# A two-layer hybrid decoder trunk: epilogues run one tile ahead, attention with a deeper lookahead, expert stages interleaved

## What is computed

```python
for l in range(2):
    sh1, sc1, g1, sh2, sc2, g2 = split(silu(c) @ ada_w[l] + ada_b[l])
    h = x * (1 + sc1) + sh1
    y = even_mixer(h) if l % 2 == 0 else odd_mixer(h)
    x = layer_norm(ALPHA * x + (1 + g1) * y)
    h = x * (1 + sc2) + sh2
    y = grouped_moe(h)          # 16 experts, top 2 of one group, d_ff 512
    x = layer_norm(ALPHA * x + (1 + g2) * y)

# even_mixer: concat(diff_attention, hgrn2) @ w_out;  odd_mixer: concat(rg_lru, stick_breaking) @ w_out
def diff_attention(q, k, v, lam, gain):      # 4 heads, two score maps per head, causal, ALiBi
    p = softmax(q @ k.T * scale - slope * dist)
    a = p[0] - lam * p[1]
    return rms_norm(a @ v, gain)

def grouped_moe(h):                           # every expert is computed, weighted by its gate
    for e in range(16):
        y += gates[:, e] * ((silu(h @ w_gate[e]) * (h @ w_up[e])) @ w_down[e])
```

## Time and profile before

| | us |
|---|---|
| five executions, median | 17749.61 |
| lowest and highest of them | 17496.92 and 18180.02 |
| the profiled execution | 17749.61 |
| its span (first to last instruction), slowest core 1 | 17748.1 |
| spans of the other cores | 17541.1 to 17740.6 |
| mean granted clock, cores 0 to 3 and 4 to 7 | 0.709 and 0.719 |

### The profile page before, as it was taken

How to read it: one execution, slowest core, us unless ns; L and a number is a source line. 1 busy time by engine, 2 the same in 40 slices (tenths; PEclk the granted TensorE clock), 3 DMA queues, 4 the chain that set the end, 5 groups by cost and what they waited for, 6 DMA issues and landing times.

```text
span 17748.1 us, 176812 instructions; the slowest of 8 cores (17541.1 to 17748.1 us)
## 1 busy us (share of the span) xinstructions
PE 12155.7 (68%) x42368; PEld 4591.4 (26%) x42368; DVE 6999.8 (39%) x11532; ACT 4772.7 (27%) x8362; POOL 3427.5 (19%) x3132
## 2 busy tenths in 40 slices
PE   5936666532958769497337678777844958949597
PEld 2311111311424334243113111111112423424243
DVE  1112222443333433333231677777743333333334
ACT  3233333300111111110431566666601111111111
POOL 0021111321222212122120122121121212212122
PEclk7967776765978878687568555555556868868798
DMA  5210000222433333232101000000012323323233
GB/s 113 81 57 8 8 1 8 80 66 58 72 68 60 58 64 58 50 65 50 54 6 39 17 9 1 8 2 8 2 65 59 64 62 53 50 63 59 63 60 60
DMA packets 603199, 811.71 MB, mean 46 GB/s; under 512 B 105994, under 2 KB 441994, under 8 KB 597516
## 3 DMA queue, kind: packets, MB, share of 16 engines
q0 software_dynamic: 362432, 446.20, 15.6%
q1 hardware_dynamic: 239760, 354.21, 6.5%
HBM read 1105.90 MB, written 138.47 MB: 70 GB/s over the span
## 4 chain that ended last, share of the span: by engine, by line
PE 48%; DVE 16%; ACT 11%; issue 8%; DMA 8%; POOL 7%; SPq 1%; DVEq 1%; ACTq 0%; POOLq 0%
PE ps L363 48%; ACT arena L312 10%; POOL arena L317 7%; DVE arena L317 6%; DVE arena L330 5%; DMA arena<-xs 2%; DVE arena L324 2%; DVE arena L346 1%; DMA arena<-x 1%; DVE arena L350 1%; DMA arena<-ada_w 1%; DVE arena L322 1%; DVEq L195 1%; DMA arena<-arena 1%; ACT L312 1%
## 5 line engine op out<-in xcount | busy, mean ns | idle before, releaser
L363 PE MATMUL ps<-arena 128*128 128x512 bf16 (+6 forms) x41280 | 11882.1, 440 | 3540.4 <-POOL arena L317 883.9
L363 PEld LDWEIGHTS ps<-arena 128*128 128x128 bf16 (+5 forms) x41280 | 4392.9, 116 | 11045.8 <-issue 8938.8
L317 POOL TENSOR_TENSOR arena<-arena 128x512 bf16<-128x512 bf16 (+3 forms) x2368 | 2989.5, 1266 | 12566.1 <-ACT arena L312 5867.8
L312 ACT ACTIVATE arena<-ps 128x512 bf16<-128x512 f32 (+2 forms) x3520 | 2022.9, 581 | 4227.1 <-PE ps L363 2933.7
L317 DVE TENSOR_TENSOR arena<-arena,ps 128x512 f32<-128x512 f32 x4096 | 2722.8, 685 | 841.7 <-PE ps L363 676.5
L312 ACT ACTIVATE arena<-arena 128x512 bf16<-128x512 f32 (+3 forms) x3013 | 1789.8, 594 | 3122.2 <-DVE arena L317 2517.6
L317 DVE TENSOR_TENSOR arena<-ps,arena 128x512 bf16<-128x512 f32 (+2 forms) x1272 | 878.1, 690 | 3768.1 <-PE ps L363 3746.1
L368 PE MATMUL ps<-arena 128*128 128x128 f32 x1088 | 273.6, 420 | 1923.0 <-DMA arena<-xs 1196.0
L330 DVE SCALAR_TENSOR_TENSOR arena<-ps,arena 128x512 f32<-128x512 f32 x1184 | 820.2, 693 | 562.5 <-ACT arena L312 540.1
L312 ACT ACTIVATE arena<-ps,arena 128x128 f32<-128x128 f32 (+2 forms) x1152 | 523.3, 460 | 1671.3 <-PE ps L368 1010.7
L317 DVE TENSOR_TENSOR arena<-arena 128x4 f32<-128x4 f32 (+6 forms) x1447 | 518.3, 388 | 991.4 <-ACT arena L312 409.7
(11 more groups left out here) (25 smaller groups left out, 928.0 us busy)
## 6 DMA issues: line engine op xcount, KB each, us to landing
arena<-moe_w_gate POOLq DMA_DIRECT2D x128, 1024.0 KB, 9.0
arena<-moe_w_up POOLq DMA_DIRECT2D x128, 1024.0 KB, 13.7
arena<-moe_w_down POOLq DMA_DIRECT2D x128, 1024.0 KB, 17.1
arena<-xs SPq DMA_DIRECT2D x192, 512.0 KB, 3.9
xs<-arena SPq DMA_DIRECT2D x96, 512.0 KB, 2.9
arena<-x SPq DMA_DIRECT2D x64, 512.0 KB, 4.1
arena<-ada_w POOLq DMA_DIRECT2D x12, 2048.0 KB, 19.1
out<-arena SPq DMA_DIRECT2D x32, 512.0 KB
```

Of the source, the lines that this page charges most:

```text
L312: self.P.op('scalar', lambda e: e.activation(out=o, in_=i, func=func, **kw), reads=_rs([in_, bias, scale]), writes=[out.r])
L317: self.P.op(eng, lambda e: e.tensor_tensor(out=o, in0=x, in1=y, op=op), reads=_rs([a, b]), writes=[out.r])
L363: self.P.op('tensor', lambda e: e.matmul(o, l, r, start=start, stop=stop), reads=_rs([lhsT, rhs] + list(xr)), writes=[out.r])
```

## The change

Four things change; what is computed does not.

Epilogues: `epilogue` is split into a load (`xload`), `epi_t1`, `epi_sums`, `epi_norm` and `epi_out`, and `epilogue_seq` runs them over the tiles so that gate product and sums of tile i + 1 stand between normalisation and output of tile i, with loads two tiles ahead out of a ring of three tiles (`xe_pool`). The square moves from POOL to ACT. Attention: three score banks (0, 1, 7) instead of two, probabilities three key blocks ahead instead of one, five `P` tiles instead of four; and the normaliser (`finish`) of a pair of blocks is issued inside the first block of the next pair. Experts: `stage2` of the item before no longer follows `stage1` as a whole; one of its four tiles follows each group `fc`.

```diff
-    xt_pool = b.pool([128, D], F32, 2, "xt")
+    xt_tiles = [b.sb([128, D], F32, "xt") for _ in range(2)]
+    def ring(tiles):
...
+    xt_pool = ring(xt_tiles)
...
-    def epilogue(xsrc, xdst, t0, y):
-        xe = xt_pool()
+    def xload(xsrc, t0):
+        xe = xe_pool[0]()
         b.dma('sync', xe, xsrc[t0:t0 + 128, :])
+        return xe
+
+    def epi_t1(y):
         t1 = ework[0]()
...
+    def epi_sums(xe, t0, t1):
         r = ework[1]()
-        b.stt('gpsimd', r, xe, ALPHA, t1, ALU.mult, ALU.add)
-        b.tt('gpsimd', t1, r, r, ALU.mult)
+        b.stt('vector', r, xe, ALPHA, t1, ALU.mult, ALU.add)
+        b.act(t1, r, AF.Square)
...
+    def epi_norm(ctx):
+        t0, xe, t1, r, st = ctx
         b.ts('vector', t1, r, st[:, 2:3], ALU.subtract, st[:, 6:7], ALU.mult)
         b.tt('gpsimd', r, t1, lnG, ALU.mult)
...
+    def epi_out(xdst, ctx):
+        t0, xe, t1, r, st = ctx
+        b.tt('vector', xe, r, lnB, ALU.add)
+        b.dma('sync', xdst[t0:t0 + 128, :], xe)
+
+    def epilogue_seq(xsrc, xdst, tiles, produce=None):
+        n = len(tiles)
+        xes = [xload(xsrc, tiles[0]), xload(xsrc, tiles[1])]
+        ctx = epi_sums(xes[0], tiles[0], epi_t1(produce(0)))
+        for i in range(n):
+            if i + 2 < n:
+                xes.append(xload(xsrc, tiles[i + 2]))
+            t1 = epi_t1(produce(i + 1)) if i + 1 < n else None
+            epi_norm(ctx)
+            nxt = epi_sums(xes[i + 1], tiles[i + 1], t1) if i + 1 < n else None
+            epi_out(xdst, ctx)
+            ctx = nxt
...
-                a = stage1(e, ch, wcur[e])
-                if prev is not None:
-                    stage2(*prev)
-                prev = (e, ch, wcur[e], a)
-            stage2(*prev)
-            for i in range(TH // 128):
-                epilogue(xsrc, xdst, tok0 + i * 128, yacc[:, i, :])
+                gbs, actT = stage1_begin(e, ch)
+                for fc in range(4):
+                    stage1_fc(e, ch, wcur[e], gbs, actT, fc)
+                    if prev is not None:
+                        stage2_tile(*prev, fc)
+                prev = (e, ch, wcur[e], actT)
+            for ti in range(4):
+                stage2_tile(*prev, ti)
+            epilogue_seq(xsrc, xdst, [tok0 + i * 128 for i in range(TH // 128)], lambda i: yacc[:, i, :])
...
-        p_pool = b.pool([128, 512], BF16, 4, "Pa")
+        p_pool = b.pool([128, 512], BF16, 5, "Pa")
...
+        pend = []
+
+        def finish(o, sq, h, qs):
+            ss = bank(6)
+            b.mm(ss, onesf, sq)
+            rstd = rl_pool()
+            b.rsqrt(rstd, ss, 128e-6, rstd)
+            b.stt('vector', BIG[:, h, qs], o, dgS, rstd, ALU.mult, ALU.mult)
...
-                        st = bank(J % 2)
+                        st = bank((0, 1, 7)[J % 3])
...
-                    P = s1(0)
-                    for J in range(nJ):
-                        Pn = s1(J + 1) if J + 1 < nJ else None
-                        b.mm(OT, vv[:, J, :], P, J == 0, J == nJ - 1)
-                        b.mm(LT, onesb, P, J == 0, J == nJ - 1)
-                        P = Pn
+                    Ps = {}
+                    for J in range(-3, nJ):
+                        if J + 3 < nJ:
+                            Ps[J + 3] = s1(J + 3)
+                        if J >= 0:
+                            P = Ps.pop(J)
+                            b.mm(OT, vv[:, J, :], P, J == 0, J == nJ - 1)
+                            b.mm(LT, onesb, P, J == 0, J == nJ - 1)
+                            if pend and J == min(6, nJ - 1):
+                                finish(*pend.pop())
...
-                ss = bank(6)
-                b.mm(ss, onesf, sq)
-                rstd = rl_pool()
-                b.rsqrt(rstd, ss, 128e-6, rstd)
-                b.stt('vector', BIG[:, h, qs], o, dgS, rstd, ALU.mult, ALU.mult)
+                pend.append((o, sq, h, qs))
+        finish(*pend.pop())
```

More of the change, by code:

```diff
@@ L488, in build, with nxt @@
     b.pop()
-    xt_pool = b.pool([128, D], F32, 2, "xt")
+    xt_tiles = [b.sb([128, D], F32, "xt") for _ in range(2)]
+    def ring(tiles):
+        k = [0]
+        def nxt():
+            k[0] += 1
+            return tiles[(k[0] - 1) % len(tiles)]
+        return nxt
+    xt_pool = ring(xt_tiles)
     hf_pool = b.pool([128, 8, 128], F32, 2, "hf")
@@ L574, in moe_sublayer @@
         r1 = b.pool([128, 1], F32, 8, "r1")
+        xe_pool[0] = ring(xt_tiles + [b.sb([128, D], F32, "xe")])
         def router(hf, col):
@@ L671, in stage1 @@
-                return actT
-            def stage2(e, ch, wts, actT):
-                wd = wts[2]
-                for ti in range(4):
-                    ycnt[0] += 1
-                    ya, yb = (PS[3][0], PS[3][1]) if ycnt[0] % 2 else (bank(4), bank(5))
-                    for nh, yp in ((0, ya), (1, yb)):
-                        for fc in range(4):
-                            b.mm(yp, actT[:, fc, ti * 128:(ti + 1) * 128], wd[:, fc, nh * 512:(nh + 1) * 512],
-                                 fc == 0, fc == 3)
-                    tix = ch * 4 + ti
-                    for nh, yp in ((0, ya), (1, yb)):
-                        ys = yacc[:, tix, nh * 512:(nh + 1) * 512]
-                        if e == 0:
-                            b.cp('vector', ys, yp)
-                        else:
-                            b.tt('vector', ys, ys, yp, ALU.add)
+                return gbs, act_pool()
@@ new lines, in stage1_fc @@
+            def stage1_fc(e, ch, wts, gbs, actT, fc):
+                wg, wu, wd = wts
+                c0 = ch * 512
+                pg, pu = bank(2 * (fc % 2)), bank(2 * (fc % 2) + 1)
+                for kc in range(8):
+                    b.mm(pg, wg[:, kc, fc * 128:(fc + 1) * 128], BIG[:, kc, c0:c0 + 512], kc == 0, kc == 7)
+                for kc in range(8):
+                    b.mm(pu, wu[:, kc, fc * 128:(fc + 1) * 128], BIG[:, kc, c0:c0 + 512], kc == 0, kc == 7)
+                s_ = s_pool()
+                b.act(s_, pg, AF.Silu)
+                tg = t_pool()
+                b.tt('vector', tg, pu, gbs, ALU.mult)
+                b.tt('gpsimd', actT[:, fc, :], s_, tg, ALU.mult)
@@ new lines, in stage2_tile @@
+            def stage2_tile(e, ch, wts, actT, ti):
+                wd = wts[2]
+                ycnt[0] += 1
+                ya, yb = (PS[3][0], PS[3][1]) if ycnt[0] % 2 else (bank(4), bank(5))
+                for nh, yp in ((0, ya), (1, yb)):
+                    for fc in range(4):
+                        b.mm(yp, actT[:, fc, ti * 128:(ti + 1) * 128], wd[:, fc, nh * 512:(nh + 1) * 512],
+                             fc == 0, fc == 3)
+                tix = ch * 4 + ti
+                for nh, yp in ((0, ya), (1, yb)):
+                    ys = yacc[:, tix, nh * 512:(nh + 1) * 512]
+                    if e == 0:
+                        b.cp('vector', ys, yp)
+                    else:
+                        b.tt('vector', ys, ys, yp, ALU.add)
@@ L730, in outproj_epilogue, with produce @@
         wo = b.sb([128, 8, D], BF16, "wo")
+        xe_pool[0] = ring(xt_tiles + [b.sb([128, D], F32, "xe")])
         b.dma('gpsimd', wo, wout.re("(k p) n -> p k n", p=128))
-        for ti in range(NT):
+        def produce(ti):
             ya, yb = PS[2 + ti % 2][0], PS[2 + ti % 2][1]
@@ L736, in outproj_epilogue @@
                     b.mm(yp, BIG[:, kc, ti * 128:(ti + 1) * 128], wo[:, kc, nh * 512:(nh + 1) * 512], kc == 0, kc == 7)
-            epilogue(xsrc, xdst, ti * 128, (ya, yb))
+            return (ya, yb)
+        epilogue_seq(xsrc, xdst, [ti * 128 for ti in range(NT)], produce)
     def stop_at(tag):
```

21 lines of the change are left out of this document (4 added, 17 removed).

## The result

| | before | after |
|---|---|---|
| median of the runs, us | 17847.49 (17 runs) | 16474.29 (10 runs, 16067.73 to 16703.86) |
| ratio, 95% interval | | 0.9133 (0.9046 to 0.922) |
| the profiled execution | 17749.61 | 16081.11 |
| span, slowest core | 17748.1 (core 1) | 16079.6 (core 0) |

The account below looks back on a forecast made before the run. Matmuls bound the expert main loop; waits, not an engine, bound epilogues and attention. Savings of 738 (epilogues) plus 506 (attention) less 30 (expert-loop clock), 1214, from 17749.6 gave 16,536, rounded 16,530 us; range 16,250 to 16,900.

Parts of the forecast that it names:

- Epilogue, predicted 738: Epilogues run one tile ahead: 364 us saved behind the experts and 374 behind the two projections.
- POOL's 2.34 us multiply now runs beside VectorE's multiply-add ... I take 1.2: Epilogue: running beside POOL's multiply costs VectorE 1.2 us a tile, the middle between 0 and 2.34.
- the allowance for small operations and gaps: Epilogue tile: 0.8 us of small operations and some 0.5 between dependent ones, within VectorE's 8.1.
- Attention, predicted 556 less 50: Attention: 139 us saved per head, 556 for four heads, less half of up to 100 for the clock, giving 506.
- The 50 charged for 0.81: Attention: dense stretches granted a clock of 0.81 instead of 1.00 cost up to 100 us; half was taken.
- The blocks of 4, set at 0: Attention blocks of 4 key blocks: no gain, bound by reciprocal and masks, the first by a new head's loads.
- 6 x 7.7 less 1.2: Attention first blocks: 7.7 us more each from the normaliser's wait (9.2 less 1.5), less 1.2 in the block of 12.
- the 13 in the blocks of 8: Attention blocks of 8 key blocks: 13.0 and 14.3 us instead of 15.6 and 24.7, a gain of 13 per head.
- Expert loop, predicted -30: Expert main loop: reorder gains 0; 30 us charged, between 0 and 100, for a lower clock after shorter epilogues.
- A: Rival: attention stays at 1.2 GHz, saving 168 us there instead of 506; about 16,870 us; chance 0.12.
- B: Rival: expert loops fall to a clock of 0.81 everywhere, 616 us more; about 17,120 us; chance 0.11.
- C: Rival: interleaved expert loop makes TensorE wait at every second-stage tile, 1.6 us each; 18,170 us, slower; chance 0.03.

Follow-up runs that it names:

- experiment 4: Changed kernel with the normaliser issued at once, lookahead of 3 kept: 16,152.06 us; changed kernel with a lookahead of 1, normaliser still put off: 16,766.79 us.
- experiment 3: Interleaved expert order alone on the kernel before: 17906.39 us against 17685.36; changed kernel with the plain order: 16176.65, and on one chip 16212.92 against the changed kernel's 16188.39.

## Why the prediction was right, step by step

- *Epilogue, predicted 738, measured 957.* Behind the two projections the first to the last multiply-add took 492.9 and 485.3 us, now 244.9 and 244.5: 489. Behind the experts it is 988 less 520: 468. (By its own figures a tile behind a projection is 9.7, not 9.8, some 6 us in all; it measured 7.9.) The chain was right: one tile ahead, loads covered, VectorE the bound, no table load (181 as in the earlier trace rows). The step that was mis-sized is "POOL's 2.34 us multiply now runs beside VectorE's multiply-add ... I take 1.2". It cost VectorE 0 and POOL 0.8, so two of the signs of being right, tiles 9 to 10 us apart and a multiply-add well above 1.22, did not come. The reading behind it, "the row shows both slowed", missed that they were slowed in turn: each line of the earlier trace rows merges two instructions. The first two, apart (kernel before, core 1):

```profile
3251.69 1.16 POOL L317 TENSOR_TENSOR arena<-arena 128x512 bf16<-128x512 f32 x1 [5.41 <-DVE arena L330]
3252.07 1.32 DVE L317 TENSOR_TENSOR arena<-arena 128x512 bf16<-128x512 f32 x1 [0.65 <-ACT arena L312]
```

  POOL's, begun first, took 1.16, about what its masks over 512 columns take in the earlier trace rows (1.15); VectorE's, begun 0.38 later, took 1.32 where some 0.7 was its own. The working treated an exclusion with an order as a rate. The other 0.7 of 9.5 against 7.6 is the allowance for small operations and gaps, which ran closer together; times 128 tiles it is 90 us.
- *Attention, predicted 556 less 50, measured 605* (first to last reciprocal, 1877 us on core 1 before, 1273 on core 0 after). Block by block the working held. Gains in us, predicted and measured (mean of cores and heads):

| key blocks | 4 | 8 | 12 | 16 | 20 | 24 | 28 | 32 |
|---|---|---|---|---|---|---|---|---|
| first block | 0 / -0.8 | 13 / 13.3 | 11.5 / 12.7 | 13.4 / 13.9 | 14.1 / 15.1 | 14.8 / 16.0 | 15.5 / 17.3 | 16.2 / 17.4 |
| second block | 0 / 2.8 | (both) | 5.0 / 4.2 | 5.7 / 5.8 | 6.4 / 6.8 | 7.1 / 7.5 | 7.8 / 9.5 | 8.5 / 10.5 |

  In sum 139 against 152 a head. The 50 charged for 0.81 did not show on the cores that kept 1.00 in the dense stretches, core 0 among them: their long second blocks gained more than the working, not less. It did show on cores 2 and 3, which were at 0.81 for some 620 us of the heads (a stretch of core 2 below): 1309 and 1306 us from first to last reciprocal, where the other six had 1264 to 1273.

```profile
2404.00:2434.00 30.00, 27.52 (x100) 10.43 (x98) 9.65 (x11) 19.59 (x34) 6.09 (x6) 0.81 0.00 1
```

  The blocks of 4, set at 0, gave 2.0. Putting the normaliser off was priced at 6 x 7.7 less 1.2, so 45, and a share of the 13 in the blocks of 8; experiment 4 gives 52.
- *Expert loop, predicted -30.* The reorder is worth nothing at a given clock (experiment 3). In the profiled executions the slowest cores' loops were 148 us shorter after (5927 on core 1, 5779 on core 0), so the charge had the wrong sign there; that the change made them shorter is not shown, as one kernel's loops differ by nearly as much (5557 us on the mean of the cores in this profile of the changed kernel, 5696 in its other one). Together 957 + 605 + 148 = 1710, where the spans, of two different cores, differ by 1668.5. On the mean of the eight cores the first two are 960 and 608, and everything outside the half loops fell by 1558, from 11,835 to 10,277.
- *Rivals.* A fell: 0.83 in the heads and 0.65 an exponential. C fell: 708 us a loop. B, all loops at 0.81, did not come, but in 13 of the 14 profiled executions some core had some of its loops longer than the 680 us of the full clock, before as after. With all its loops at full clock a core of the changed kernel took 15,650 us (core 5 of the profile), with five of the eight partly at a lower one 16,043 and 16,080 (cores 1 and 0). The range's lower end, 16,250, was too high for the second chip (16,188).

## What to carry to other kernels

Where two engines run side by side for the first time, ask of the nearest row which of the two was issued first before taking a rate from it, and look at single instructions, as a merged line hides the answer: here the order made the whole difference between 0 and 1.63 us a tile on the engine that bounds. A chain of small waits is priced well by walking it in the timeline, block size by block size; that is also how the next gain (diagonals and heads' starts) was found. And where the clock of a long dense stage differs from execution to execution, compare kernels by stages at the same granted clock, and on one chip. An engine that seems to stand still for nothing may be working through waits that the kernel's own recorder wrote.

## What the runs showed that was not expected

In the expert loops two cores of a pair (0 with 1, 2 with 3, and so on) share the granted clock. Windows of the changed kernel's profile, cores 0, 2 and 3 of one die and core 4 of the other, all four cores of each in their loops (times count from each core's own first instruction):

```profile
core 0: us, PE busy (x) PEld busy (x) DVE busy (x) ACT busy (x) POOL busy (x), PEclk, DMA share, GB/s
4000.00:4100.00 100.00, 99.21 (x440) 43.86 (x448) 38.44 (x56) 13.09 (x22) 26.28 (x25) 1.00 0.53 88
...
core 2: us, PE busy (x) PEld busy (x) DVE busy (x) ACT busy (x) POOL busy (x), PEclk, DMA share, GB/s
4000.00:4100.00 100.00, 100.00 (x369) 40.07 (x368) 30.91 (x46) 11.30 (x19) 22.37 (x22) 0.81 0.33 54
core 3: us, PE busy (x) PEld busy (x) DVE busy (x) ACT busy (x) POOL busy (x), PEclk, DMA share, GB/s
4000.00:4100.00 100.00, 100.00 (x372) 40.29 (x370) 31.92 (x47) 10.71 (x18) 20.71 (x19) 0.81 0.35 59
core 4: us, PE busy (x) PEld busy (x) DVE busy (x) ACT busy (x) POOL busy (x), PEclk, DMA share, GB/s
4000.00:4100.00 100.00, 99.69 (x449) 43.84 (x448) 37.22 (x54) 13.69 (x23) 25.83 (x24) 1.00 0.52 87
```

Cores 2 and 3 have 0.81 where 0 and 1 have 1.00; some 1700 us later (5700 to 5800) it is 0.86 for cores 0 and 1 and 1.00 for 2 and 3; cores 4 to 7 have 1.00 in both. In every profile here the loops of two cores of a pair agree within about 1%, those of two pairs differ by up to 15%. The Trainium skill (TensorE: Matmul & The Clock Gate, Seeing it yourself) has a die fall to 13/16 as a whole once three of its cores are dense; these rows show the level but not that rule, as a pair is held back alone and a die with four dense cores is not. That the cores of different pairs started at the same moment no row shows; but in the kernel with the 768-column reduction all eight cores kept the full clock in all eight half loops (5427 to 5432 us). What decides it was not found: the mean of the eight half loops over the cores of a profile went from 5430 us (that kernel, in that execution) to 5950 (lookahead of 1), in no order with the stages' lengths or the matmuls' order. Another execution of the first of these took 16,499 us, with cores 0 to 3 at 0.733 to 0.735, so it is not settled by the kernel alone. This stays open.
